# Loading X first, the last residual in token rows, and the latents' norms made under the last projection units

## The reference

```
for each layer:
  x += 0.5 * rms(SwiGLU_1(rms(x, g0)), g1)          # d_ff 2816
  hn = rms(x, g2);  p = hn @ w_in                   # 10 units of 256 columns
  cq, ckv = rms(p.cq, q_norm), rms(p.ckv, kv_norm)  # 256 and 128 wide
  kpe = rope(p.kpe)                                 # 32 wide
  mla = latent attention, 8 heads, chunk causal; the streams attend to 512 cached rows too
  mlstm, hgrn2 = two recurrent mixers, 4 heads each, from the other columns of p
  x += rms(concat(mla, mlstm, hgrn2) @ w_out, g3)
  x += 0.5 * rms(SwiGLU_2(rms(x, g4)), g5)
outputs: x (y_prompt, y_sample) and the new states and caches
```

## Time and profile before

| what | us |
|---|---|
| median of 3 runs | 2848.92 (2848.05 to 2851.24) |
| profiled execution | 2850.88 |
| its span, first to last instruction | 2849.1 |
| PE busy | 2729.6 (96%) |
| DVE, ACT, POOL busy | 1250.8, 899.2, 381.5 |

### The profile page before, as it was taken

How to read it: one execution, slowest core, us unless ns; L and a number is a source line. 1 busy time by engine, 2 the same in 40 slices (tenths; PEclk the granted TensorE clock), 3 DMA queues, 4 the chain that set the end, 5 groups by cost and what they waited for, 6 DMA issues and landing times.

```text
span 2849.1 us, 45143 instructions
## 1 busy us (share of the span) xinstructions
PE 2729.6 (96%) x18648; PEld 2611.4 (92%) x18648; DVE 1250.8 (44%) x1701; ACT 899.2 (32%) x1220; POOL 381.5 (13%) x346
## 2 busy tenths in 40 slices
PE   6999999998899999999999999999989999999997
PEld 6999999995679999999999999999856889999997
DVE  3333333635756633233363323354466746332334
ACT  4221223415644422122342212233264433221222
POOL 0110011102135011001101001110122330100110
PEclk9999999999999999999999999999999999999999
DMA  3223222320015222321322232142101152223212
GB/s 114 74 65 88 79 63 77 96 54 10 18 40 87 65 83 59 89 74 57 91 60 74 68 85 78 53 104 78 28 8 31 37 104 62 78 69 86 75 55 70
DMA packets 367940, 191.19 MB, mean 67 GB/s; under 512 B 36478, under 2 KB 363473, under 8 KB 367823
## 3 DMA queue, kind: packets, MB, share of 16 engines
q1 hardware_dynamic: 363822, 179.07, 23.4%
q0 software_dynamic: 4000, 10.47, 1.5%
HBM read 183.58 MB, written 5.93 MB: 67 GB/s over the span
## 4 chain that ended last, share of the span: by engine, by line
PE 87%; DVE 6%; ACT 3%; issue 2%; DMA 1%; SPq 1%; ACTq 0%; DVEq 0%
PE ps L587 25%; PE ps L588 25%; PE ps L589 25%; PE ps L826 2%; DVE w L1728 1%; PE ps L835 1%; DMA raw<-in_w_out_dram 1%; ACT w L1256 1%; PE ps L954 1%; PE ps L886 1%; PE ps L932 1%; PE ps L868 1%; DVE at L2003 1%; DVE y L1821 1%; PE ps L933 0%
## 5 line engine op out<-in xcount | busy, mean ns | idle before, releaser
L587 PE MATMUL ps<-xh,w 128*128 128x320 f32 x3456 | 1077.4, 312 | 25.8 <-DVE xl L1805 17.3
L589 PE MATMUL ps<-xh,w 128*128 128x320 f32 x3456 | 1072.1, 310 | 0.0
L588 PE MATMUL ps<-xl,w 128*128 128x320 f32 x3456 | 1072.1, 310 | 0.0
L587 PEld LDWEIGHTS ps<-xh,w 128*128 128x128 f32 x3456 | 652.5, 189 | 35.5 <-DVE xl L1805 23.9
L588 PEld LDWEIGHTS ps<-xl,w 128*128 128x128 f32 x3456 | 652.7, 189 | 0.3
L589 PEld LDWEIGHTS ps<-xh,w 128*128 128x128 f32 x3456 | 652.5, 189 | 0.0
L1728 DVE TENSOR_TENSOR w<-raw,w 128x2048 fp32r<-128x2048 f32 x172 | 400.1, 2326 | 382.9 <-ACT w L1256 382.8
L1256 ACT ACTIVATE w<-raw 128x2048 fp32r<-128x2048 f32 (+2 forms) x185 | 342.6, 1852 | 457.2 <-PE ps L589 416.7
L587 PE MATMUL ps<-hh,w 128*128 128x320 f32 x1408 | 437.4, 311 | 1.0 <-DVE w L1728 1.0
L589 PE MATMUL ps<-hh,w 128*128 128x320 f32 x1408 | 435.1, 309 | 0.0
L588 PE MATMUL ps<-hl,w 128*128 128x320 f32 x1408 | 435.1, 309 | 0.0
(11 more groups left out here) (355 smaller groups left out, 2664.0 us busy)
## 6 DMA issues: line engine op xcount, KB each, us to landing
raw<-in_w_ffn_in_dram SPq DMA_DIRECT2D x178, 512.0 KB
raw<-in_w_ffn_out_dram SPq DMA_DIRECT2D x64, 384.0 KB
raw<-in_w_ffn_out_dram SPq DMA_DIRECT2D x64, 320.0 KB
raw<-in_w_in_dram SPq DMA_DIRECT2D x38, 512.0 KB
raw<-in_w_out_dram SPq DMA_DIRECT2D x12, 512.0 KB
out_dram<-xio SPq DMA_DIRECT2D x5, 512.0 KB
xio<-in_x_prompt_dram SPq DMA_DIRECT2D x1, 2048.0 KB
y<-in_cache_ckv_dram POOLq DMA_DIRECT2D x8, 256.0 KB, 3.2
```

The source lines that it names most:

```text
L587: pe.matmul(out, wh, xh, start=first, stop=False)
L588: pe.matmul(out, wh, xl, start=False, stop=False)
L589: return pe.matmul(out, wl, xh, start=False, stop=last)
```

## The change

- **Start.** The identity and X are loaded first, on their own semaphore, into another place (XIN); TensorE spins, then waits for these three loads only, and takes the parameters between chunks 4 and 5. Chunks are evicted in turn, even ones by DVE, odd ones by ACT, three ahead. ACT splits the second weight unit between X's pieces; the small lower-bound computations come after them.
- **Preparation.** TensorE swaps the rope keys inside unit 7, sums CQ's squares at the start of unit 8 and CKV's at the start of unit 9, in banks that these units leave free. ACT makes the squares at unit 6 and Ln and Exp at units 8 and 9; DVE rotates the keys before it drains unit 7 and scales the latents before it drains unit 9. After unit 9 TensorE starts with head 0's queries and keys, then the transposes, VM and the convolution states; DVE evicts VM. The first two decays and products go into the loop (steps 0, 3 and 4, 6), the memsets of QPE to POOL, HGG's silu and gain behind the streams. POOL copies the rotated keys before it makes distances.
- **End.** In the last unit no squares are summed. TensorE transposes X tile by tile, with the sums of squares as single columns (one for each token tile) after tile 2, then Y times its gain (YG, made by ACT). DVE evicts X tiles 0, 2 and 4, ACT 1 and 3; DVE then computes Y tile * 1/rms + X tile in token rows, and SP stores them.

```diff
+            (IDENT[:, :], A["c_ident"]),
+            (XIN[:, 0:PT_, :], A["x_prompt"][0].rearrange("(t p) f -> p t f", p=P)),
+            (XIN[:, PT_, :], A["x_sample"].rearrange("b t f -> (b t) f")),
+        ):
+            sp.dma_start(dst, src).then_inc(x_in, 16)
...
+        def finish(l, u):
...
+            pe.wait_ge(drained, u + 2)
+            for t in range(TILES):
+                if t >= 2:
+                    pe.wait_ge(*((xt_act, KD // 2 + t // 2) if t % 2 else (xio_sb, KD // 2 + t // 2)))
+                turned(END_X[t], t, X)
+                if t == 2:
+                    pe.wait_ge(*sq_added.nth(l, ADD * 2 + KD - 2))
+                    pe.wait_ge(*sq_ready.nth(l, SQ_POST[2] + KD))
+                    for n in range(TILES):
+                        cut = slice(n * P, (n + 1) * P)
+                        for k, squares in enumerate((SY, GB[:, 0, :], GB[:, 1, :])):
+                            mm = pe.matmul(PS[:, 2, n:n + 1], squares[:, cut], ONES[:, 0:1], start=k == 0, stop=k == 2)
+                    mm.then_inc(ms_ready.sem, 1)
+            pe.wait_ge(gained, KD)
+            for t in range(TILES):
+                if t == 0:
+                    pe.wait_ge(drained, u + 3)
+                elif t == 1:
+                    pe.wait_ge(xt_act, KD // 2 + 2)
+                elif t == 2:
+                    pe.wait_ge(xio_sb, KD // 2 + 3)
+                else:
+                    pe.wait_ge(xio_sb, KD // 2 + 3 + t - 2)
+                turned(END_Y[t], t, YG)
...
+                    if i == 1:
+                        norm_sums(l, j)
                     for t in range(TILES):
+                        if i == 0 and j == 1 and t in (0, 2):
+                            swapped_keys(l, 1 - t // 2)
...
+        def swapped_keys(l, h):
...
+            else:
+                pe.wait_ge(drained, unit(l, PROJ, 0, 6) + 3)
+            held(pe)
+            mm = pe.matmul(PS[:, 3 + 4 * h, 0:HALF], SWAP, MISC[0:QK, h * HALF:(h + 1) * HALF], start=True, stop=True)
+            if h == 0:
+                mm.then_inc(kswap_ps.sem, 1)
...
+        def norm_sums(l, j):
+            if j == 0:
+                pe.wait_ge(*mla_sq.nth(l, 0))
+                pe.wait_ge(*kpe_ready.nth(l, 0))
+                for h in range(2):
+                    for c in range(2):
+                        mm = pe.matmul(PS[:, 3 + 4 * h, 0:HALF], ONES[:, :], GB[:, c, h * HALF:(h + 1) * HALF],
+                                       start=c == 0, stop=c == 1)
+            else:
+                pe.wait_ge(*mla_r.nth(l, 0))
+                for h in range(2):
+                    mm = pe.matmul(PS[:, 3 + 4 * h, 0:HALF], ONES[:, :], R[:, h * HALF:(h + 1) * HALF],
+                                   start=True, stop=True)
+            mm.then_inc(mla_ms.sem, 1)
...
+            pe.wait_ge(drained, unit(l, PROJ, 0, 8) + 3)
+            pe.wait_ge(*cq_ready.nth(l, 0))
+            for half in range(2):
+                head_queries(l, 0, half)
+            pair_keys(l, 0)
+            pe.wait_ge(*kper_zero.nth(l, 0))
             held(pe)
+            for t in range(TILES):
+                pe.transpose(PS[:, 7, t * QK:(t + 1) * QK], KPER[0:QK, t * P:(t + 1) * P], IDENT[0:QK, 0:QK])
+            pe.wait_ge(drained, unit(l, PROJ, 0, 9) + 3)
...
+        pe.wait_ge(dve_setup, 1)
+        spin(PS[:, 7, :], 6)
+        pe.wait_ge(x_in, 16 * 3)
         for c in range(KD):
-            if c >= 4:
-                pe.wait_ge(xio_sb, c - 3)
+            if c >= 3:
+                pe.wait_ge(xt_act if c % 2 == 0 else xio_sb, (c - 3) // 2 + 1)
+            if c == 5:
+                pe.wait_ge(setup_in, 16 * SETUP_LOADS)
+                pe.transpose(PS[:, 6, 0:96], PROW[0:96, 0, :], IDENT[0:96, 0:96])
+                pe.transpose(PS[:, 6, 96:146], PROW[0:50, 1, :], IDENT[0:50, 0:50])
+                pe.matmul(PS[:, 6, 256:256 + LAYERS * DK], ONES[0:1, :], HROW[:, :], start=True, stop=True)\
+                    .then_inc(xio_ps, 1)
...
+            for c in range(KD - 1):
+                gain_of_y(c)
+            square_last(l, 2, 0, u)
+            square_last(l, 2, 1, u)
+            gain_of_y(KD - 1)
+            tile_of_x(1)
+            act.wait_ge(*ms_ready.nth(l, 7))
+            chain.link(run(RT, PS[:, 2, 0:TILES], ACT.Ln, bias=EPSC, scale=1.0 / D))
+            run(RT, RT, ACT.Exp, scale=-0.5).then_inc(r_ready.sem, 1)
+            tile_of_x(3)
...
+                if n == 6:
+                    act.wait_ge(*xl_ready.nth(l, SPLIT_PRE[1] + NPC - 1))
+                    act.wait_ge(drained, unit(l, PROJ, 0, 5) + 3)
+                    act.wait_ge(*rt_ps.nth(l, 0))
+                    run(GB[:, :, :], CQ[:, :, :], ACT.Square)
+                    run(R[:, :], CKVT[:, :], ACT.Square).then_inc(mla_sq.sem, 1)
...
+                if n >= 8:
+                    act.wait_ge(*mla_ms.nth(l, n - 8))
+                    r = GB[:, n - 8, :]
+                    for h in range(2):
+                        ins = run(r[:, h * HALF:(h + 1) * HALF], PS[:, 3 + 4 * h, 0:HALF], ACT.Ln, bias=EPSC[:, 0:1],
+                                  scale=1.0 / (QL, KVL)[n - 8])
+                    chain.link(ins)
+                    run(r, r, ACT.Exp, scale=-0.5).then_inc(mla_r.sem, 1)
...
-                if n in (13, 21):
-                    decays(l, 2 if n == 13 else 3)
+                if n in (0, 3, 13, 21):
+                    decays(l, (0, 3, 13, 21).index(n))
...
+        x_in_place(1)
+        x_in_place(3)
         split_hi(0, 0, 0, 0)
-        split_hi(0, 0, 0, 1)
-        for c in range(KD):
-            act.wait_ge(xio_ps, c + 2)
-            run(X[:, c, :], psf[:, (c % 4) * 1024:(c % 4) * 1024 + T], ACT.Copy).then_inc(xio_sb, 1)
-        act.wait_ge(dve_setup, 5)
+        x_in_place(5)
+        act.wait_ge(dve_setup, 4)
+        for n in range(NPC):
+            if n == 2:
+                x_in_place(7)
+            if n == 4:
+                split_hi(0, 0, 0, 1)
...
+            last_half(l, 2, 0)
+            last_half(l, 2, 1)
+            for t in range(0, TILES, 2):
+                dve.wait_ge(xio_ps, KD + t + 2)
+                V.tensor_copy(XIO[:, t, :], PS[:, END_X[t]:END_X[t] + 2, :].rearrange("p b n -> p (b n)"))\
+                    .then_inc(xio_sb, 1)
+            dve.wait_ge(*r_ready.nth(l, 7))
+            dve.wait_ge(xio_sb, KD // 2 + 3)
+            for t in range(TILES):
+                dve.wait_ge(xio_ps, KD + TILES + t + 2)
+                if t % 2:
+                    dve.wait_ge(xt_act, KD // 2 + t // 2 + 1)
+                V.scalar_tensor_tensor(out=XIO[:, t, :],
+                                       in0=PS[:, END_Y[t]:END_Y[t] + 2, :].rearrange("p b n -> p (b n)"),
+                                       scalar=RT[:, t:t + 1], in1=XIO[:, t, :], op0=ALU.mult, op1=ALU.add)\
+                    .then_inc(xio_sb, 1)
...
+                if n == 7:
+                    rotated_keys(l)
+                if n == 9:
+                    scaled_latents(l)
...
-            scaled(l, 0)
-            scaled(l, 1)
...
+            for t in range(PT_):
+                dve.wait_ge(*v_ps.nth(l, t))
+                V.tensor_copy(VM[:, t, :], PS[:, 3 + t, :]).then_inc(v_sb.sem, 1)
...
+                if n in (4, 6):
+                    scaled(l, n // 2 - 2)
```

More of the change, by code:

```diff
@@ L628, in last_unit @@
         def last_unit(l, stage, u, n, w, parts, xh, xl):
+            final = stage == 2 and l == LAYERS - 1
             begin(u)
@@ L637, in last_unit, with turned @@
                                    xh[:, k, cut], xl[:, k, cut], k == 0, k == n - 1)
-                    if h and k == 1:
+                    if h and k == 1 and not final:
                         sum_squares_y(l, stage, 0, 0, 1 if stage == 1 else 2)
-                    if h and k == n - 4:
+                    if h and k == n - 4 and not final:
                         sum_squares_y(l, stage, 0, 1 if stage == 1 else 2, 3)
                 mm.then_inc(unit_done if h else unit_half.sem, 1)
-            sum_squares_y(l, stage, 1, 0, 3)
+            if final:
+                finish(l, u)
+            else:
+                sum_squares_y(l, stage, 1, 0, 3)
+        def finish(l, u):
+            def turned(bank, t, src):
+                for c in range(KD):
+                    at = bank * 512 + c * P
+                    mm = pe.transpose(psf[:, at:at + P], src[:, c, t * P:(t + 1) * P], IDENT[:, :])
+                mm.then_inc(xio_ps, 1)
+            pe.wait_ge(drained, u + 2)
[22 more added lines that the diff above has]
+                turned(END_Y[t], t, YG)
         def sum_squares_x(l, pre):
@@ L959, in mla @@
             mla_prep(l)
-            for half in range(2):
-                head_queries(l, 0, half)
-            pair_keys(l, 0)
             attend_scores(l, 0)
             attend_scores(l, 1)
+            pe.wait_ge(*cn_sb.nth(l, 0))
             head_queries(l, 1, 0)
@@ L1601, in mla @@
```

(25 more changed lines are left out.)

288 lines of the change are left out of this document (133 added, 155 removed).

## The result

The changed kernel takes **2805.52 us** (median of 3 runs, 2804.14 to 2806.67), the kernel before 2848.92: ratio 0.9844, 95% interval 0.9825 to 0.9864. Forecast were 2805.9, range 2799 to 2818. The profiled execution took 2806.67 us, its span 2804.8, against 2850.88 and 2849.1 before. The 44.3 us between the spans can be followed by marks, instructions that both profiles have (the first matmuls, DVE's low parts of the units' weights, the drains, the attention loop's maxima).

| stretch | predicted | by the marks |
|---|---|---|
| start, up to the 25th matmul of unit 0 | 9.7 | 10.2 |
| preparation and loop, layer 0 | 12.2 | 13.5 |
| preparation and loop, layer 1 | 12.9 | 14.2 |
| end | 8.2 | 6.2 |
| stretches that the change does not touch | 0 | +1.8 -3.2 -1.7 +1.6 +1.6 = 0.1 |

A forecast was written before the change was run, and what follows sets the result against it. TensorE (87% of the span) was taken as bound by waits between dense stretches; separate gains of 9.7 (start), 25.1 (preparation and loop, both layers) and 8.2 (end) sum to 43.0 us: median 2805.9, range 2799 to 2818.

The forecast's parts named there:

- Start, 9.7: Up to unit 1's first matmul: X's own semaphore and shared evictions gain 9.7 us, bounds 7 and 11.
- The estimate with the Trainium skill's figures: X's load: about 2.0 us fixed plus bytes at 436 GB/s, making the start's sum about 1 us better.
- the next stop: After the FFN's start, unit 1 waits for W1, whose low part DVE ends at 27.2 us.
- Inserted products, 4.3: Projection units 7 to 9: 16 added TensorE passes cost 4.3 us per layer, on the path.
- Moved waits, 0: Units 7 to 9: inserted products wait 0 for ACT and DVE; DVE's scalings end about 2 us before unit 9.
- rival D: Projections: in-order queues of unit 9's drain and the norms form a ring, TensorE idles, clock falls; slower, chance 0.03.
- First score, 10.8 after the drain: After the projections, the first attention score comes 10.8 us after unit 9, instead of 29.66 and 30.33.
- Loop, 2 (and 0.4 for the queries): Attention loop: moved decays and products cost 2 us per layer (between 0 and 4.7); queries waiting for ACT's conv copies, 0.4.
- idle thirds: Attention loop: ACT and DVE each have about a third idle, so most of the moved work fits.
- Rival A: Attention loop: moved work delays every engine, all 4.7 per layer, and gates wait 3 for stores; 2817 us, chance 0.15.
- End, 8.2: After the last unit: fewer sums, X transposed first and DVE's five Y additions gain 8.2 us, bounds 5 and 10.
- Rival B: Tail: one-column sums and transposes let the clock fall, TensorE paces Y tiles; 4.5 us, 1.5 at the start; 2812, chance 0.09.

The follow-up runs named there:

- r3: The changed kernel with the old start: all loads on one semaphore, parameters first, ACT alone evicting X, low parts after all of X; 2815.49 us.
- r1: The changed kernel run again as it is, with a second profile; 2805.96 us, ratio 0.983.
- r4: The changed kernel with both latent norms' sums, their Ln and Exp and DVE's three scalings back behind unit 9; 2819.5 us.
- r10: The changed kernel with the attention loop's two pairs of decay products made by GpSimd instead of DVE; 2806.7 us, ratio 0.9838.
- r12: r11 with GpSimd's products of r10 and the second decay moved behind the copies that the next pair's keys wait for; 2796.22 us, ratio 0.9804.
- r7: The changed kernel with DVE's two pairs of decay products at steps 7 and 11 of the attention loop instead of 4 and 6; 2807.87 us.
- r9: The new tail of r8, but again with 15 one-column sums on TensorE instead of 5; 2804.44 us, ratio 0.9827.
- r8: The changed kernel with another tail: GpSimd adds the last squares (5 one-column sums, not 15), X tiles in three pairs of banks; 2797.52 us, ratio 0.9809.
- r11: r8 with 34 unused products ahead of X instead of 6, and the last residual divided among ACT, GpSimd and DVE; 2800.59 us, ratio 0.982.

## Why the prediction was right

- **Start, 9.7: right**, 9.5 to 9.8 by r3 (10.2 between the first two profiles). X's release (10.6; 10.54 to 10.94 measured) and the low level of the first 25 transposes (all of them in the first profile, a part in r1, where they took 4.30) hold; the FFN's start came 0.8 sooner than forecast (22.75; 21.91), and the parameters took 0.9, not 1.45, as the clock was up by then. The estimate with the Trainium skill's figures (DMA: Bandwidth & Descriptors, section Anatomy of one DMA) would have had X in 1 us sooner; the two loads landed 8.1 and 9.0 us after their issue, and the section's fit is for DMAs that GpSimd issues, while SP issues these. What did not hold is the next stop: W1's low part was done at 25.7 for the forecast 27.2, and unit 1 never waited for it. Unit 1 stood at 27.07 for the forecast 27.2 to 28.1 because unit 0 ran at the low level; two ways to nearly one number, and so this part of the start is luck.
- **Inserted products, 4.3: right**, 4.25 and 4.23. **Moved waits, 0: right**; the cover behind DVE's scalings was 2.55, not 2, and rival D's ring of waits did not close. r4 prices the move of the norms at half of the preparation's gain.
- **First score, 10.8 after the drain: 10.2.** V began 5.4 after it, not 5.95.
- **Loop, 2 (and 0.4 for the queries): 1.75 in all**, 0.76 up to the second maximum, where the queries wait for the convolution copies, and 0.99 from there to the ninth. The size was nearly right, the reason half right: I had counted ACT's and DVE's work against idle thirds, while one 1.04 us instruction in front of a copy goes with the 0.99, and 2.7 us on DVE made none of it as long as that instruction stood there (r10, r12). Rival A had the right place and the wrong price.
- **End, 8.2: 6.2 in the first profile and in r7, 7.5 to 8.3 in the six others with this tail (8.0 in r1).** The step that failed is the full clock in the tail. At the full clock tiles 3 and 4 take 1.9, and they took 3.45; the last sums were 0.8 longer, the first Y tile later by about 0.5: 2.9 in the first profile, of which shorter sums (3.3 at the full clock for 3.8), additions (1.21 for 1.27) and store (3.5 for 3.9) give 1.2 back. Rival B had priced the same terms at 4.5 and one wrong: DVE still paced the Y tiles. Its cause is not the one it named, by r9. The Trainium skill (TensorE: Matmul & The Clock Gate, section PE-mode transpose) says that the full clock doesn't engage for transposes, which don't count as busy in the same way. r8 disagrees, as the earlier trace rows did: its tail is 80 transposes and five sums in 10.3 us, and the granted clock reads 1.00 until they end.
- **The sum** came within 0.4 us of the median (1.2 of the profiled execution) because misses cancel, which is luck: the start (0.5) and the preparation with the loop (2 x 1.3) were 3.1 better and the end 2.0 worse, with 0.1 from stretches that nobody touched but that hold single items of 1.6 to 3.2. The forecast's own range, 2801 to 2812, is the fair measure of what was known.

## What to carry to other kernels

Sum each stretch as its own chain, and for work moved into a busy loop look for the one instruction that then stands ahead of a copy others wait for; idle shares say little. Compare two profiles by marks along the span, since single executions of one kernel differ by 1.5 to 3 us at places that no edit touches. Unused products ahead of TensorE's work behind a long load have to last until the load lands: 34 did and brought the third unit 0.5 to 1.5 us forward, 21 left 3.4 us idle and brought nothing that can be told from chance.

## What the runs showed of the hardware

- The granted clock's column read 1.00 in the first 20 us of the first profile, though 25 transposes took 0.22 us each; with 21 spins ahead, when they took 4.62 in all, the column was below 1 in the windows from 10 to 16 us (0.77, 0.50, 0.88), and with 34 they took 0.12 each. So a 1.00 in the column at the start of a profile has to be checked against durations.
- Low stretches come at the same handful of places (the norms around 500 and 1410, in the loops near 704 and 2088, behind the mixers near 900, 930 and 2316), but none of these in every profile: 7.8 to 23.3 of low clock in the eleven kernels made from the changed one.
- DVE's scaling of 128 x 640 took 0.84 us alone and 1.5 beside GpSimd's subtractions (r4). GpSimd's two copies of 64 x 512 took 2.41 in the kernel before, beside three such scalings (1.0, 1.0 and 1.2), and 1.17 in the changed order.
- From the last tile's producer to the end of the span it was 3.5 us when the tile before had been ready 1.2 us earlier, and 4.25 when it had been ready 0.4 us earlier (r11; 4.2 in r12); each store is 0.5 MB.
